# Who makes the low halves of the weights during the merges: a two-block fp32 network on one NeuronCore

## The reference, cut to what matters

```python
h = rmsnorm(x, attn_norm_g[l])
parts = split(h @ w_in[l], split_points)
branches = (mla_branch(...), shortconv_branch(...), dsa_branch(...), gla_branch(...))
merged = sum(sigmoid(gate_pre[n]) * (branches[n] @ w_branch[l, n]) for n in range(4))
x = x + merged @ w_out[l]
h2 = rmsnorm(x, ffn_norm_g[l])
x = x + (silu(h2 @ w_ffn_gate[l]) * (h2 @ w_ffn_up[l])) @ w_ffn_down[l]
```

## Time and profile before

| | |
|---|---|
| median of 3 runs | 2375.38 us (2374.11 to 2378.97) |
| profiled execution, its own time | 2374.26 us |
| its span, first to last instruction | 2372.5 us |
| PE busy | 2295.4 us (97%) |
| DVE busy | 1816.8 us (77%) |
| ACT busy | 1331.8 us (56%) |
| POOL busy | 495.8 us (21%) |
| granted TensorE clock, mean | 0.991 of full |

### The profile page before, as it was taken

The page is one execution under the profiler, slowest core; times in us unless marked ns, Lnnn a source line. Parts: engine busy times, 40 slices in busy tenths (PEclk is TensorE's granted clock), DMA queues, the critical chain, the costliest instruction groups (busy, mean ns, idle before and its releaser), DMA issues.

```text
span 2372.5 us, 51374 instructions
## 1 busy us (share of the span) xinstructions
PE 2295.4 (97%) x19294; PEld 2211.3 (93%) x19294; DVE 1816.8 (77%) x3486; ACT 1331.8 (56%) x2309; POOL 495.8 (21%) x628
## 2 busy tenths in 40 slices
PE   8999999999999999999999999989999998999998
PEld 8998899899999999899899999888999998899998
DVE  7688857688876688966788887688887658888764
ACT  6665556756555655556766554655554465556443
POOL 0000003717930000001635951710000026000000
PEclk9999999999999999999999999999999999999999
DMA  6533343345555543343345555433555544345553
GB/s 236 167 120 110 117 146 125 117 151 166 175 176 172 167 142 111 114 143 132 117 145 172 174 180 170 143 129 122 173 183 186 185 157 143 127 150 181 186 185 132
DMA packets 99989, 363.52 MB, mean 153 GB/s; under 512 B 11824, under 2 KB 12336, under 8 KB 99504
## 3 DMA queue, kind: packets, MB, share of 16 engines
q1 hardware_dynamic: 99344, 360.31, 45.9%
q10 hardware_dynamic: 416, 0.08, 0.0%
HBM read 359.29 MB, written 1.05 MB: 152 GB/s over the span
## 4 chain that ended last, share of the span: by engine, by line
PE 58%; DVE 25%; DVEq 6%; ACT 5%; issue 4%; ACTq 1%; DMA 0%; SPq 0%
PE psum L474 57%; DVE ring_lo L1405 5%; ACT arena L911 2%; DVE arena L1457 2%; DVE arena_r L1393 1%; DVE arena L1449 1%; DVEq L1915 1%; ACT ring_hi L924 1%; DVE arena_r L1391 1%; DVEq L1385 1%; DVE arena L1631 1%; PE psum L546 1%; DVE arena L1628 1%; DVE arena L1465 1%; DVE arena L1853 1%
## 5 line engine op out<-in xcount | busy, mean ns | idle before, releaser
L474 PE MATMUL psum<-hn_hi,ring_hi 128*128 128x272 f32 (+2 forms) x3696 | 1080.8, 292 | 24.9 <-DVE ring_lo L1405 15.6
L474 PE MATMUL psum<-hn_hi,ring_lo 128*128 128x272 f32 (+2 forms) x3696 | 1053.2, 285 | 0.0
L474 PE MATMUL psum<-hn_lo,ring_hi 128*128 128x272 f32 (+2 forms) x3696 | 1051.7, 285 | 0.0
L924 ACT ACTIVATE ring_hi<-ring 128x1024 fp32r<-128x1024 f32 x678 | 707.8, 1056 | 188.9 <-DMA ring<-w 158.4
L2165 POOL TENSOR_TENSOR ring_lo<-ring,ring_hi 128x256 fp32r<-128x256 f32 x616 | 488.7, 830 | 1424.5 <-ACT ring_hi L924 1424.2
L1405 DVE TENSOR_TENSOR ring_lo<-ring,ring_hi 128x1024 fp32r<-128x1024 f32 x524 | 641.3, 1233 | 160.8 <-ACT ring_hi L924 126.6
L474 PEld LDWEIGHTS psum<-hn_hi,ring_hi 128*128 128x128 f32 x3696 | 698.3, 189 | 48.4 <-issue 22.9
L474 PEld LDWEIGHTS psum<-hn_lo,ring_hi 128*128 128x128 f32 x3696 | 699.4, 189 | 1.8
L474 PEld LDWEIGHTS psum<-hn_hi,ring_lo 128*128 128x128 f32 x3696 | 698.3, 189 | 0.0
L474 PE MATMUL psum<-arena_r,ring_hi 128*128 128x256 f32 (+2 forms) x3380 | 622.9, 285 | 12.6 <-DVE ring_lo L1405 10.6
L911 ACT ACTIVATE arena<-psum 128x272 f32<-128x272 f32 (+7 forms) x736 | 257.5, 367 | 554.5 <-PE psum L474 469.1
(11 more groups left out here) (172 smaller groups left out, 1509.0 us busy)
## 6 DMA issues: line engine op xcount, KB each, us to landing
ring<-w SPq DMA_DIRECT2D x678, 512.0 KB, 3.3
cst<-consts SPq DMA_DIRECT2D x1, 1960.0 KB, 13.1
x_sb<-x_meta SPq DMA_DIRECT2D x2, 544.0 KB, 4.3
out<-x_sb SPq DMA_DIRECT2D x1, 1024.0 KB, 3.9
arena<-lam SPq DMA_DIRECT2D x1, 256.0 KB, 6.2
par_sb<-par SPq DMA_DIRECT2D x1, 185.0 KB, 6.5
pos_sb<-positions SPq DMA_DIRECT2D x1, 128.0 KB, 6.0
cst<-consts ACTq DMA_DIRECT2D x1, 66.0 KB, 6.0
```

The costliest lines, as they stand in the source:

```text
L474: i = nc.tensor.matmul(out_, lhsT=lhsT, rhs=rhs, start=first, stop=last)
L924: nc.scalar.activation(ring_hi[:, slot], ring[:, slot], ACT.Copy).then_inc(slab_hi[k % RING], 1)
```

## The change

The end of POOL's part in each layer of block 2 moves from the end of the front to the end of the last merge. `KT` is 8, so `FRONT` goes from 184 to 504 blocks, and POOL's slabs in a layer from 17 to 57. 40 slabs a layer, 80 in all, go from DVE's L1405 (one instruction each) to POOL's L2165 (four each). Nothing else in the code changes.

```diff
-FRONT = 184
+FRONT = 184 + 4 * KT * (KT + 2)
 POOL_SLABS |= {k for layer in range(DEPTH) for at in [DEPTH * BLOCKS1 + layer * BLOCKS2]
                for k in range(at // SLAB + AHEAD_SLABS, (at + FRONT) // SLAB)}
```

## The result

| | before | after |
|---|---|---|
| median (8 runs each, same chip) | 2375.36 us | 2383.02 us (2380.93 to 2386.31) |
| ratio, 95% interval | | 1.0038 [1.0026, 1.005] |
| span of the profiled execution | 2372.5 us | 2380.7 us |
| granted clock, mean | 0.991 | 0.989 |

The change makes the kernel slower: by 0.38% by the ratio, and by 7.7 us (0.32%) between the two medians. The forecast was 2373.0, a gain of 2.4 us; the time lies in the range of 2361 to 2385, on the side that had a chance of 0.25.

What follows compares the result with a forecast made beforehand. TensorE, busy 97% of the span, was taken as the bound, with VectorE setting the pace in A and B. A -4.0 and -3.0, B +1.6 twice, D +1.0 twice, clock -0.6: -2.4 us, 2373.0, range 2361 to 2385.

Steps and rivals of the forecast that it cites:

- Part 1: 40 low halves a layer leave VectorE; PE's waits for them go: -4.0 and -3.0 in A, -2.8 in B.
- A: First layer's stretch 1549.3 to 1599.0, first merge with attention of branch 0; PE gains 4.0 us, 3.0 in second layer.
- The mean of 0.29: Average extra us per VectorE instruction with two SBUF operands beside GpSimd, from three lines; the forecast took 0.35.
- B: Stretch behind A, to 1645.0 in the first layer: eight masked sums and second merge; forecast +1.6 us a layer.
- Part 2: VectorE's two-operand SBUF instructions lengthen beside GpSimd; masked sums in B come late: -2.8 + 4.4 = +1.6 us a layer.
- the 2.2 twice: PE's forecast waits for late masked values in B, 2.2 us at each of the two pairs of heads.
- D: First layer's stretch to 1707.0: last merge, products alone, PE sets the pace; forecast +1.0 us a layer.
- Part 3: Whether GpSimd keeps up: in D it falls behind, about 1.0 us late at the end, once a layer.
- Part 4: Second layer's low granted clock from 2012 to 2016 may go with the wait for a low half: -0.6 us.
- Rival 2: Port paid at its dense price throughout: 0.45 us an instruction in B, 3.72 a slab in D; 2383, chance 0.18.
- Rival 1: Low-half waits were the whole cost, longer masked sums hidden, GpSimd keeps its lead: 2361.6 to 2362.8, chance 0.27.
- Rival 3: Full exclusive hold: first three masked sums 9.8 us longer, +10 us a layer on the forecast, 2392; chance 0.05.

Runs made afterwards that it cites:

- e1: Against the kernel before: 40 merge low halves a layer off VectorE, GpSimd subtracts only 16 columns for each, result left incomplete; 2356.2 us.
- e8: Against the kernel before: GpSimd makes only the first four merge low halves of each layer; 2369.59 us.
- e12: Against the kernel before: GpSimd makes seven chosen merge slabs a layer (1st to 4th, 9th, 10th, 19th); 2368.85 us.
- e4: Against the kernel before: GpSimd makes the 30 low halves a layer of the second to fourth merge, VectorE keeps the first merge's; 2380.04 us.
- e2: Kernel before with VectorE keeping all merge low halves, plus four unused GpSimd subtracts of constants beside each merge slab; 2450.48 us.
- e10: Against the kernel before: GpSimd makes the merge slabs from the fifteenth on, 26 a layer; 2380.54 us.
- e11: Against the kernel before: GpSimd makes only the 20 low halves a layer of the last two merges; 2380.7 us.
- e7: Changed kernel with each GpSimd merge slab in eight subtracts of 128 columns in place of four of 256; 2391.72 us.
- e13: Against the kernel before: GpSimd makes only the merge slabs from the 25th on, 16 a layer; 2371.08 us.

## Why the prediction came out wrong

**Part 1 failed, in its step for A.** "A -4.0 and -3.0": from the end of the front (L2016) to L2093 the layers lost 4.1 and 4.5 us. That the three waits for low halves go was right. What failed is "VectorE gains 7 us, more than the 4.0 that PE can use". It was a balance of busy time, 14.5 removed against 7.4 added, and both sides were wrong:

- *The removed work was partly filler.* 6.2 us of the 14.5 came back as waits for ScalarE. Low halves that stand in such a gap cost the chain nothing before, so it gains nothing when they go; e1, with the same 7.1 us of waits, shows that this part has nothing to do with GpSimd. The view that tells it was there: VectorE waits only 0.9 us for ScalarE in A although each head sends it a maximum and takes back an exponential.
- *The added cost was 12.1 us, not 7.4.* The 19 two-operand instructions paid 9.1 us, 0.48 each where I had 0.35 x 0.8 = 0.28; the 13 scalar ones 3.0, 0.23 each in place of 0.16. The mean of 0.29 over L2029, L2021 and L2034 mixed instructions that stand among PSUM forms with others. L1449 and L1457 are chains of seven and eight with nothing between them, and the row nearest to them was L2029, which paid 0.445.
- *And it isn't spread.* 3.5 us of it fall in one place, right before L1885 in the order, where PE follows VectorE within 0.1 us already in the kernel before. The prediction asked that question only for the masked sums in B.

The experiments bear this out: no loss in A where the differences and factors are left alone (e8, e12), a wait behind the factors in place of the differences where only they are hit (e4), and the wait with the low halves still on VectorE (e2). How much each error weighs follows from e1. The waits alone leave VectorE a gain of 14.5 - 6.2 = 8.3 us, PE then never waits in A, and the 9.5 us between e1's 32.3 and the changed kernel's 41.8 are the price of GpSimd's work. But by the prediction's own 7.4 the 8.3 would have left only 0.9, and the 12.1 alone only 2.4 of the 14.5: either error takes the gain below the 4.0 that PE could use.

**Part 2, B: the mechanism was right.** The forms grew as said, beside GpSimd by 0.26 us for L1473 and L1468, 0.24 for L1470 and 0.20 for L1917: 9.8 us over 40 instructions, where 43 were put at 12.0. The waits for low halves (2.8) went, and the new ones are smaller than the 2.2 twice: behind a drain 1.2, L1466 0.2, and in issue (time in which the profile shows nothing that PE waited for) 5.4 where it was 3.7, together 6.8 us against 7.5. B to D gained 1.0 us in the first layer; the sum had +2.6. In the second the waits are the same size, but the granted clock is 0.66 from 2070 to 2080 where before it stays at 1.00. From L2093 to L1923 PE is busy 2.3 us longer there (105.4 us, 103.1 before) and idle 0.3 less, and that is the +2.0. e10 and e11 show that this balance is a thin one: with VectorE's low halves kept in A, so that PE comes to B without a delay from there, GpSimd's slabs make B to D 3 to 5 us longer.

**Part 3, D: not there.** PE never waits for GpSimd:

```profile
L2165 POOL TENSOR_TENSOR ring_lo<-ring,ring_hi 128x256 fp32r<-128x256 f32 x30 | 23.2, 808 | 0.9 <-ACT ring_hi L924 0.9
```

A slab takes 4 x 808 ns = 3.2 us, under the 3.3 given as the bound below which nothing is late. VectorE paid instead (L1923 749 ns, L1917 566), and it has room there. e7 shows the mechanism at 4.5 us a slab, with its waits for L2168, and e13 that the last 16 slabs cost nothing. The term was also added up wrongly: 4.9 us of falling behind less a lead of 3.6 is 1.3 us, not 1.0 (and 3.8, not 3.3, with 3.72 us a slab), which would have put the forecast at 2373.6.

**Part 4, clock: wrong in sign.** The wait for a low half went, and from 2012 to 2016 the granted clock is 1.00 in the changed kernel. But the longer wait for L1885 is followed by 6.3 us at the lower level in the first layer's A, which keeps PE busy 2.34 us longer there, nearly half of that layer's loss; in the second layer 0.50 and 0.69 from 2028 to 2036 follow it. It is a consequence of part 1 and wasn't priced with it: PE's new wait of 6.0 us brought 2.3 us more in clock in the first layer.

**The rivals.** Rival 2 gave 2383 and the kernel takes 2383.02, but not for its reasons: the dense price of 0.45 us was about right and was paid in A, which it left at -3.5 a layer, while B and D, where it put +7.5, came out near even. Rival 1 is what e1 does (-16.9, where it counted 12.6 to 13.8; from L2016 to L2093 e1 gains 6.6 and 5.1 us and behind that 3.9 and 2.4, more than PE's waits for low halves in each, and the rest was not traced). Rival 3 is refuted as a price: a full quarter of 0.75 us on top would make L1457 1.18 us by estimate; it takes 0.94. By the Trainium skill ("SBUF — State Buffer", section "Who interferes with whom") the one that comes second waits for the whole of the other's instruction. The part of that rule that spares instructions with at most one input in SBUF, outside the two-port modes, agrees here for L1465, which reads PSUM (625 ns; 623 before), and for L1893 (408 ns; 410 before). L1904, a scalar operation with one tensor in SBUF, isn't spared (718 ns; 349 before); in which mode it ran no trace here shows. The rule's direction, a high price for chains of two-operand instructions, was the warning that this case needed.

## What to carry to other kernels

Before work is taken off an engine, look whether it stood in that engine's waits: only what stands outside them shortens the chain, so subtract from the busy time what will turn into waiting. When GpSimd takes over work beside VectorE, price each dense chain of two-operand SBUF instructions at the densest row there is and ask at that very place who waits for its end; a mean over a stretch hides it. Slabs then go to GpSimd by place, by what VectorE runs while GpSimd makes them (which can be well before they are used): 7 well placed slabs a layer gained 4.2 us here and 23 gained 4.9, where all 40 lost 7.7.

## What the runs showed of the hardware

**The hold goes by GpSimd's columns, and a part of each GpSimd instruction lies outside it.** 2 ns a column holds VectorE: 0.51 us of a quarter that takes 0.75 alone. The rest, some 0.24 us, is about what e1's subtract of 16 columns takes in all (266 ns), and the same is left of 128x512, of which two alone take 2.54 us. That this rest holds nothing is worked out from these lengths and not seen by itself.

**VectorE can be kept out for many GpSimd instructions.** In e7's second layer, rows of VectorE, GpSimd and PE's loads:

```profile
2034.09 12.10 DVE L1906 TENSOR_SCALAR arena<-arena,small 128x128 f32<-128x128 f32 x2
...
2029.55 16.29 POOL L2168 TENSOR_TENSOR ring_lo<-ring,ring_hi 128x128 fp32r<-128x128 f32 x39
...
2046.27 0.50 PEld L548 LDWEIGHTS psum<-cst,arena 128*128 128x128 f32 x3 [8.81 <-DVEq L1387]
```

One of the two L1906 lasts 11.8 us (the line's shortest takes 286 ns), for as long as GpSimd issues its subtracts without a gap. It then ends, and PE has waited 8.8 us for it. A smaller case is in the changed kernel, L1962 in the front: 2.0 us once and 0.47 once, where its four instances take 0.92 to 1.12 in the kernel before. Why taking turns fails there and holds for L1457 was not tried.

**The same wait doesn't always cost the clock.** In the second layer's B PE is idle 2.58 us of the 10 from 2054 to 2064 before, and 2.39 of the 10 from 2060 to 2070 in the changed kernel. Behind that the granted clock stays at 1.00 in the first and is 0.66 over the next 10 us in the other. What decides it these runs don't tell.
